# Two layers with feed-forwards in seven products: the weight ring's places given back after the products that read the slab itself, and the second layer's memory keys computed at two entries of the first layer

## The reference

```python
h = layer_norm(ALPHA * x + 0.5 * swiglu(x, ffn1_w_gu, ffn1_w_down), ...)      # feed-forward 1, d_ff 2816
... = split(h @ w_in)                                                         # 25 slabs of weights
o_dn, o_sw = deltanet_branch(...), sliding_window_attention(...)
o_xa = memory_cross_attention(xa_q, mem_n, w_mem_kv)   # k, v = split(mem_n @ w_mem_kv): keys and values
merged = sum(sigmoid(gates) * branches @ w_branch)
h = layer_norm(ALPHA * h + merged @ w_out, ...)
x = layer_norm(ALPHA * h + 0.5 * swiglu(h, ffn2_w_gu, ffn2_w_down), ...)      # feed-forward 2
```

## Time and profile before

| | |
|---|---|
| median of 3 runs | 3284.77 us (3282.89 to 3284.87) |
| the profiled execution's own time | 3286.88 us |
| its span in the trace | 3285.1 us |
| PE busy | 3029.7 us (92%) |
| DVE busy | 1937.5 us (59%) |
| ACT, POOL busy | 644.6 us (20%), 607.8 us (19%) |
| mean granted clock of PE | 0.985 of full speed |
| the two hybrid layers end | at about 1620 us |

### The profile page before, as it was taken

One profiled execution on the slowest core, in us unless ns is written; L12 is line 12 of the kernel. 1 busy time (PEld: TensorE's weight loads), 2 busy tenths in 40 slices (PEclk: granted clock), 3 DMA queues, 4 the chain that ended last, 5 costly groups with the idle time before them and its releaser, 6 DMA issues.

```text
span 3285.1 us, 34940 instructions
## 1 busy us (share of the span) xinstructions
PE 3029.7 (92%) x13098; PEld 2016.4 (61%) x13098; DVE 1937.5 (59%) x4473; ACT 644.6 (20%) x1581; POOL 607.8 (19%) x558
## 2 busy tenths in 40 slices
PE   8999999998999999999999888888989988888877
PEld 8947997894975899788586433333338643333322
DVE  7743533775763533310263877777766487777775
ACT  1113121110101223111154111111214421111110
POOL 0010000101001000000011433434421134444442
PEclk9999999999999999999999999999999999999999
DMA  5543223453443322364334999999993499999998
GB/s 222 180 153 129 103 90 128 154 182 139 169 178 141 128 90 103 141 236 161 115 116 181 421 422 421 412 415 419 412 402 116 155 422 421 420 413 418 415 415 354
DMA packets 114937, 830.38 MB, mean 253 GB/s; under 512 B 12880, under 2 KB 13136, under 8 KB 14160
## 3 DMA queue, kind: packets, MB, share of 16 engines
q0 software_dynamic: 73728, 536.90, 39.5%
q1 hardware_dynamic: 39456, 281.29, 23.6%
q10 hardware_dynamic: 1584, 9.95, 0.8%
HBM read 827.05 MB, written 1.05 MB: 252 GB/s over the span
## 4 chain that ended last, share of the span: by engine, by line
PE 64%; DMA 23%; DVE 8%; issue 5%; ACT 1%; POOL 0%; POOLq 0%; DVEq 0%; SPq 0%; ACTq 0%
DMA arena<-table_uv,idx 22%; PE bank L344 10%; PE bank L437 9%; PE bank L2404 8%; PE bank L491 6%; PE bank L679 5%; PE bank L371 4%; PE bank L424 3%; PE bank L915 3%; PE bank L2091 2%; PE bank L2276 2%; DVE arena L2985 1%; DMA ring<-stream 1%; DVE diag L2993 1%; PE bank L577 1%
## 5 line engine op out<-in xcount | busy, mean ns | idle before, releaser
L2404 PE MATMUL bank<-arena,diag 128*128 128x512 f32 x2048 | 1017.2, 623 | 189.6 <-DVE diag L2993 182.7
L2404 PEld LDWEIGHTS bank<-arena,diag 128*128 128x128 f32 x2048 | 360.2, 192 | 722.9 <-DVE diag L2993 457.4
L2985 DVE CUSTOM_DVE_ANT_0 arena<-arena 128x1024 f32<-128x1024 f32 x512 | 625.5, 1222 | 260.9 <-DMA arena<-table_uv,idx 257.4
L3069 POOL DMA_INDIRECT arena<-table_uv,idx x512 | 535.0, 1045 | 941.8 <-PE bank L2404 726.5
L1771 POOL TENSOR_TENSOR x_tok<-arena,ktail 128x1024 f32<-128x1024 f32 (+1 forms) x12 | 27.3, 2276 | 1571.3 <-ACT arena L943 1571.3
L2641 ACT ACTIVATE dots<-dots 128x1 f32<-128x1 f32 x512 | 103.8, 203 | 1089.8 <-DVE dots L2985 1089.4
L344 PE MATMUL bank<-x,ring 128*128 128x256 f32 x1440 | 316.9, 383 | 0.0
L344 PEld LDWEIGHTS bank<-x,ring 128*128 128x128 f32 x1440 | 276.2, 192 | 39.9 <-issue 1.9
L2993 DVE TENSOR_SCALAR diag<-cst,dots,soft 128x128 f32<-128x128 f32 x512 | 175.6, 343 | 0.0
L679 PE MATMUL bank<-x,ring 128*128 128x256 f32 x768 | 173.1, 379 | 0.0
L679 PEld LDWEIGHTS bank<-x,ring 128*128 128x128 f32 x768 | 143.2, 190 | 18.8 <-issue 1.0
(11 more groups left out here) (556 smaller groups left out, 4025.7 us busy)
## 6 DMA issues: line engine op xcount, KB each, us to landing
ring<-stream SPq DMA_DIRECT2D x258, 1024.0 KB, 4.8
arena<-table_uv,idx POOLq DMA_INDIRECT x512, 13.0
ktail<-ln_rows ACTq DMA_DIRECT2D x6, 1024.0 KB, 5.7
arena<-mem_rows SPq DMA_DIRECT2D x2, 1024.0 KB, 9.6
arena<-stream SPq DMA_DIRECT2D x2, 1024.0 KB, 6.8
sq<-keys ACTq DMA_DIRECT2D x2, 1024.0 KB, 4.8
cst<-consts SPq DMA_DIRECT2D x1, 1547.0 KB, 8.1
cst<-consts SPq DMA_DIRECT2D x1, 1089.0 KB, 14.1
```

The source lines that it names most:

```text
L2404: last = mm(bank[4 + 2 * tt + half][:, :], diag[:, n % DIAGS, :], row_slot(n)[:, D + 512 * half:D + 512 * half + 512], start=(h == 0 and k ...
L2985: v.tensor_tensor_reduce(u, u, tok[:, tt, :], 1.0, 0.0, ALU.mult, ALU.add, dots[:, tt, k:k + 1]).then_inc(u_used.sem, 1)
L3069: g.indirect_dma_start(out=row_slot(n), out_offset=None, in_=peer_uv, in_offset=bass.IndirectOffsetOnAxis(ap=idx[:, h % 2, tt, k:k + 1], a ...
```

## The change

1. **Up projection.** For j > 0 the product straight from the slab comes first in `both_tiles` and raises `slab_done` there; for j = 0 it is fourth. A new count, `gu_done`, is raised at the last of the five products; ACT's copy, and DVE's sums where they take a buffer over, wait for that in place of `slab_done`.
2. **Down projection.** The order within a slab is 1, 2, 3, then 6, 5, 7, 4, and `slab_done` is raised at product 3. In the tail, products 1, 2, 3 run slab by slab and give w = 8 and w = 9 back there; then 6, 5, 7, 4 run over the three slabs, and w = 10 is given back at product 5 of w = 8. The sums of w = 10 are waited for only before its product 6. Slab 0 keeps an order of its own (3, 2, 6, 7, 4, 1, 5). DVE, where it takes a down slab's buffer, waits for one slab more, since `slab_done` no longer says that the sums were read.
3. **Norm.** `norm_by_seven` takes the accumulators up in the new order (`ACC_AT`, `done`); its last wait is a count of its own, no longer the slab's.
4. **Keys of layer 1.** Their two slabs move in the stream: one ahead of layer 0's feed-forward 2, one ahead of layer 1's feed-forward 1. PE multiplies each there, into bank 7 (`next_keys`), ACT copies it out. Behind layer 1's feed-forward 1 the two slabs of values are left, with tile 1's transposes between them. The number of slabs is the same, so is the number of matmuls.

```diff
-FFN1_AT = 0
-MEM_AT = FFN1_AT + GU_SLABS + DOWN_SLABS
+FFN1_AT = (0, 2)
+MEM_AT = GU_SLABS + DOWN_SLABS
...
-FFN2_AT = OUT_AT + OUT_SLABS
+FFN2_AT = (OUT_AT + OUT_SLABS + 1, OUT_AT + OUT_SLABS)
...
+K_AHEAD_AT = (OUT_AT + OUT_SLABS, SLABS + 1)
+K_AHEAD_BANK = 7
+V_BANKS = ((2, 0), (1, 0))
...
                 def free(j):
+                    if j == W_X.index(K_AHEAD_BANK) and not first:
+                        pe.wait_ge(mem_evac.sem, mem_evac.at(1, 1 if l == 0 else 2))
...
+                    def of_slab():
+                        sum_ready(4)
+                        return product(out_y[:, 2 * P:3 * P], w[:, 3 * KC // 2:2 * KC, :], x_sum(4))
+
+                    if j > 0:
+                        of_slab().then_inc(slab_done.sem, 1)
                     product(out_y[:, 3 * P:4 * P], t_of(4), x[:, KC // 2:KC, P:T])
...
-                    product(out_x[:, 2 * P:3 * P], t_of(2), x_sum(2))
-                    sum_ready(4)
-                    product(out_y[:, 2 * P:3 * P], w[:, 3 * KC // 2:2 * KC, :], x_sum(4)).then_inc(slab_done.sem, 1)
+                    if j == 0:
+                        of_slab().then_inc(slab_done.sem, 1)
+                    product(out_x[:, 2 * P:3 * P], t_of(2), x_sum(2)).then_inc(gu_done.sem, 1)
...
+                for w in range(1, DOWN_SLABS - LAST):
+                    rows_ready(w)
+                    sums_ready(w)
+                    product(w, 1)
                     product(w, 2)
...
+                    product(w, 3).then_inc(slab_done.sem, 1)
+                    for i in (6, 5, 7, 4):
+                        product(w, i)
                 tail = range(DOWN_SLABS - LAST, DOWN_SLABS)
                 for w in tail:
-                    down_ready(w)
-                    last = product(w, 1)
-                last.then_inc(acc_done.sem, 1)
...
+                    rows_ready(w)
+                    if w < tail[-1]:
+                        sums_ready(w)
+                    for i in (1, 2, 3):
+                        last = product(w, i)
+                        if w == tail[-1]:
+                            last.then_inc(acc_done.sem, 1)
+                    if w < tail[-1]:
+                        last.then_inc(slab_done.sem, 1)
+                for i in (6, 5, 7, 4):
+                    for w in tail:
+                        if i == 6 and w == tail[-1]:
+                            sums_ready(w)
+                        last = product(w, i)
+                        if i == 5 and w == tail[0]:
+                            last.then_inc(slab_done.sem, 1)
+                    last.then_inc(acc_done.sem, 1)
...
+            def next_keys(s):
+
+                two_tiles(bank[K_AHEAD_BANK], slab(0, K_AHEAD_AT[s]), mem_n).then_inc(slab_done.sem, 1)
...
                 if seven_products(l, 1):
-                    ffn_by_seven(l, 1, FFN2_AT)
+                    next_keys(0)
+                    ffn_by_seven(l, 1, FFN2_AT[l])
+                    next_keys(1)
...
-                if i >= 3:
-                    dve.wait_ge(slab_done.sem, slab_done.at(l, slab - 2))
+                if i >= GU_SLABS + 3:
+                    dve.wait_ge(slab_done.sem, slab_done.at(l, slab - 1))
+                elif i >= 3:
+                    dve.wait_ge(gu_done.sem, gu_done.at(l, f * FC + i - 2))
...
                 by_channel(l, n, 0, x, gain, shift)
-                dve.wait_ge(slab_done.sem, slab_done.at(l, end))
+                done(7)
                 from_x(1, 0, acc(4))
```

More of the change, by code:

```diff
@@ L62 @@
 LN_BANK = 3
-ACC_AT = (0, 6, 9)
+ACC_AT = (0, 7, 10)
 def seven_products(l, f):
@@ new lines, in ffn_by_seven @@
+                sums_ready(0)
+                for i in (3, 2, 6, 7, 4):
+                    product(0, i)
+                pe.wait_ge(gu_summed.sem, gu_summed.at(l, f * FC + GU_SLABS))
+                product(0, 1).then_inc(slab_done.sem, 1)
+                product(0, 5)
+                for w in range(1, DOWN_SLABS - LAST):
+                    rows_ready(w)
+                    sums_ready(w)
+                    product(w, 1)
+                    product(w, 2)
+                    product(w, 3).then_inc(slab_done.sem, 1)
+                    for i in (6, 5, 7, 4):
+                        product(w, i)
@@ L557, in ffn @@
                 by_rows(l, 2 * f, hidden, FC, at + GU_SLABS, ready)
+            def next_keys(s):
+                two_tiles(bank[K_AHEAD_BANK], slab(0, K_AHEAD_AT[s]), mem_n).then_inc(slab_done.sem, 1)
             pe.wait_ge(x_loaded, 16)
             for l in range(DEPTH):
-                ffn_by_seven(l, 0, FFN1_AT)
+                ffn_by_seven(l, 0, FFN1_AT[l])
+                if l == 0:
+                    for s in range(2):
+                        w = slab(l, MEM_AT + s)
+                        two_tiles(bank[s], w, mem_n).then_inc(slab_done.sem, 1)
+                        if s == 0:
+                            x_waits(l, 0, 0)
+                            to_channels(l, 0, 1, y)
+                    pe.wait_ge(mem_evac.sem, mem_evac.at(l, 1))
                 for s in range(2):
-                    w = slab(l, MEM_AT + s)
-                    two_tiles(bank[s], w, mem_n).then_inc(slab_done.sem, 1)
-                    if s == 0:
+                    if l > 0 and s == 1:
                         x_waits(l, 0, 0)
                         to_channels(l, 0, 1, y)
-                pe.wait_ge(mem_evac.sem, mem_evac.at(l, 1))
-                for s in range(2):
                     w = slab(l, MEM_AT + 2 + s)
@@ L576, in tensor @@
                         for mt in range(TT):
-                            last = mm(bank[2 if mt == 0 else 0][:, :], mem_n[:, k, mt * P:mt * P + P],
+                            last = mm(bank[V_BANKS[l][mt]][:, :], mem_n[:, k, mt * P:mt * P + P],
                                       w[:, 4 * kk:4 * kk + 4, :].rearrange("p b n -> p (b n)"),
@@ L988, in ffn, with keys_of, next_keys @@
                 root_table()
+            def keys_of(s, b):
+                fn(kmem[:, 2 * s:2 * s + 2, :].rearrange("p h t -> p (h t)"), bank[b][:, :],
+                   ACT.Copy).then_inc(mem_evac.sem, 1)
+            def next_keys(s):
+                act.wait_ge(slab_done.sem, slab_done.at(0, K_AHEAD_AT[s] + 1))
+                keys_of(s, K_AHEAD_BANK)
             act.wait_ge(zeroed, 1)
```

116 lines of the change are left out of this document (52 added, 64 removed).

## The result

The changed kernel takes 3243.11 us in the median of 4 runs (3242.43 to 3243.71), the kernel before, run beside it, 3284.82 us (3282.89 to 3286.11). The ratio is 0.9872, 95% interval [0.9857, 0.9886]: 41.7 us less, where 39.5 were forecast.

A forecast was written before the change was run, and what follows sets the result against it. PE, with 64% of the chain, was taken to bound the kernel; 24.3 + 1.5 - 1.7 + 1.6 + 13.8 = 39.5 us off the 3285.1 us span gave 3245.6, forecast as 3245 us, range 3238 to 3260.

The forecast's parts named there:

- The tails, 24.3 us: Three down projection tails: PE's waits for DVE's sums and the slow stretch after them vanish, saving 24.3 us.
- Slabs behind the tails, 1.5 us: Keys behind two tails: places given back earlier let them start 0.89 us after the transposes, saving 1.5 us.
- Up projection, 0: Up projection: PE never waits in its steady part, so the earlier release saves 0.
- The entries, -1.7 and +1.6: Layer 0's feed-forward 2 entry 1.7 us longer, layer 1's feed-forward 1 entry 1.6 us shorter, keys included.
- the 4.74 I used: Slab ring: 4.74 us from a place given back until DVE can start on the new slab.
- The lock of DVE and POOL: Layer 1's entry: exclusive port lock keeps DVE's tile 1 addition ending as before; without it, some 0.75 us earlier.
- Behind layer 1's feed-forward 1, 13.8 us: After layer 1's feed-forward 1: two slabs of keys leave, 2 x 6.91 us, saving 13.8 us.
- The cover of 0.5 us for tile 1: Behind layer 1's feed-forward 1: ACT's tile 1 scaling takes 7.3 us, PE comes at 7.8; fits by 0.5 us.
- The signs that I named: Hybrid layers: no down projection waits, 18.0 us tails, clock near 1, entry waits 0.3 to 1 us, end near 1581.
- the release does not help: Rival, tails: sums of w = 10 stay the limit, the 24.3 us remain, 3269 us; chance 0.05.
- slower: Rival, up projection: turns DVE-bound; at 0.8 us wait for each of 63 slabs, 3295 us; chance 0.02.
- Part of it: Rival, entries: thinner cover, waits add up and PE's clock still falls; 3252 to 3262 us, chance 0.18.

The follow-up runs named there:

- POOL later: Against the changed kernel, POOL starts tile 1's token rows at the two entries only after DVE has written its half of `x`: 3252.93 us, ratio 0.9904.

## Why the prediction was right, step by step

- **The tails, 24.3 us**: measured 7.5 + 8.1 + 8.8 = 24.4 by starts. DVE's timeline of the changed kernel for slab 10 in the first tail, first and last sum:

```profile
203.55 0.69 DVE L1317 TENSOR_TENSOR z<-ring 128x512 f32<-128x512 f32 x1 [3.04 <-PE bank L503]
...
205.48 0.69 DVE L1322 TENSOR_TENSOR o_xa<-ring,z 128x512 f32<-128x512 f32 x1
```

  With t = 0 at 200.70 the sums run from 2.85 to 5.5 (forecast 2.6 to 5.3), for a use at 210.14, 9.4. The idle column alone would have given 14.6 plus the short waits of 2.1; reading start to start took in the slow stretch, and the runs bear that out. (The 0.857 us for a down product is not 48.08 divided by 56, which is 0.859; 21 products are 18.0 us either way.)
- **What in the change does it**: the prediction gave the steady part's release and the tail's order one term. The runs part them: the tail alone has all of it, the steady part alone leaves 2.5 us of wait three times. The early release of w = 7 wasn't needed, though by little: in the kernel with only the tail new DVE starts on slab 10 at 205.24, 0.2 us before PE reads it (205.47), where the forecast had 0.4.
- **Slabs behind the tails, 1.5 us**: 0.8 and 0.75, as forecast.
- **Up projection, 0**: shown by the kernel with it undone.
- **The entries, -1.7 and +1.6**: -2.0 and +1.3. The size of the waits was off in both. At the first, 0.6 and 0.5 us by starts in place of 0.46 and 0.35: the idle time is shorter than that, but the first row behind each wait is 0.1 us longer (2.05 and 1.16 in place of 1.95 and 1.06). At the second, the slab waited for took 1.3 us longer than the 4.74 I used (below), 1.68 us of wait in place of 0.46. It cost nothing: the slab only took the room of the two waits for DVE that I had put behind it, and the second `both_tiles` starts at 810.07, 20.4 us behind the transposes' start, as forecast. The missing 0.3 us lie inside that `both_tiles`, 4.72 us in place of 4.47; why is open.
- **The lock of DVE and POOL**, which I let hold tile 1's norm where it was: DVE's and POOL's timelines of the changed kernel at layer 1's entry:

```profile
788.82 2.23 DVE L1407 TENSOR_TENSOR arena<-arena 128x512 f32<-128x512 f32 x1
...
797.64 2.84 DVE L1320 TENSOR_TENSOR dec<-ring,dec 128x512 f32<-128x512 f32 x1
...
800.52 2.73 DVE L1322 TENSOR_TENSOR at_<-ring,dec 128x512 f32<-128x512 f32 x1
...
788.16 2.35 POOL L1811 TENSOR_TENSOR x_tok<-arena,ktail 128x1024 f32<-128x1024 f32 x1 [202.05 <-ACT arena L967]
```

  The addition to tile 1 starts 0.9 us earlier against the tail's end than in the earlier trace rows, takes 2.23 us in place of 1.35, and ends at 791.05, 1.40 us behind the transposes' start, where before it ended 1.42 behind it. Starting it sooner bought nothing: the forecast let it end where it did, and so it did. The Trainium skill, "SBUF — State Buffer", section "SBUF: two separate sides", describes this exclusive lock; the run with POOL later agrees with it (0.68 us for a sum without POOL, 2.74 and 2.83 beside it).
- **Behind layer 1's feed-forward 1, 13.8 us**: with the slab's 0.75 it makes 14.6, measured 14.7. The cover of 0.5 us for tile 1 held: the transposes at 1011.98 follow the values without a wait.
- **What the sum did not have**: 1.7 us of slow clock less from layer 0's tiny matmuls on, and 0.4 us more at the start, where the 24 matmuls of the program's first three `first_tile` took 8.15 us in place of 7.75. From the tiny matmuls to the transposes at layer 0's entry the kernel before took 326.5 us (255.94 to 582.39), the one with the keys alone too; the changed one took 324.8 (248.02 to 572.82), as did six others; the one with POOL later, the same code as the changed one up to there, took 323.1 (248.23 to 571.33). So this stretch moves in steps of 1.7 us without a change of code, and layer 1's, from the tiny matmuls to the end of the layers, does too: 561.7 us in the kernel before, the changed one and four others, 563.4 in the other four. I don't count the 1.7 us to the change. But in layer 0 the two kernels with the old tail and the old release, one trace each, are the two slowest, so the runs don't rule out that the change has a part in it.
- **How near the total came**: the trace ends at 3241.9, 3.7 us before the 3245.6 worked out. Nearly all of that lies outside the terms of the sum: 2.7 us come from the rest of the program and 1.7 from that slow clock, while the entries took 0.6 and the start 0.4 us more than forecast.
- **The signs that I named**: the waits at the third `first_tile` and before the second `both_tiles` were to be 0.3 to 1 us; they were 0.36 and 0.19 at the first entry, 1.68 and none listed at the second. The others came as named: 18.0 us in three tails, granted clock 1.00 at layer 1's entry, no wait between the values' slabs, the end of the layers at 1581.41.
- **Rivals**: "the release does not help" and "slower" are out by the tails' pace and by an up projection without waits but the one at the third slab, which was there before. "Part of it" named the right place, the entries, but its 7 to 17 us did not come: their sum is 0.6 us off the forecast.

## What to carry to other kernels

Where a ring is fed as its places come free, look at the last steps before the work changes its order: the steady loop had 4.3 us of slack here before the change (the sums of w = 7 were ready at 189.95, for a product at 194.27), and the tail, which asked for the sums of w = 10 two products after the slab was given its place, had none. Put there the products that need only the slab ahead of those that need something made from it; the early release in the steady loop and in the up projection could have stayed undone. Work that depends on nothing current costs a part of its weight (3.0 us for 12.1) if it goes where the engine waits anyhow, and gives back its full weight where it stood (14.7 us with the slab's 0.75). A lock between two engines can't be scheduled away by delaying one of them, if what the other does next meets it too and has less cover.

## What the runs showed of the hardware that was not expected

**A slab of 1 MB that took 6.0 us.** At layer 0's entry the slab behind the keys landed as usual. The transfers of the changed kernel from 583 to 591 us (engine, count, KB, us to landing):

```profile
ring<-stream SPq DMA_DIRECT2D x1, 1024.0 KB, 4.7
```

At layer 1's entry, from 796 to 806 us, it took 6.0 us, with one packet of the instruction queue in the same time (queue: packets, MB, share):

```profile
q8 instruction: 1, 0.02, 0.5%
...
ring<-stream SPq DMA_DIRECT2D x1, 1024.0 KB, 6.0
```

PE's wait for that slab was 1.64 to 1.77 us in five kernels and 1.07 and 1.49 in two others, and 0.28 to 0.45 at the other entry, so it goes with the place in the program and is no accident of one run. In all seven the slab took 5.4 to 6.1 us with such a packet in the same 10 us; with layer 1's keys left out it took 4.8, and the one packet of instructions in that window is of another queue. That the packet holds up one of the engines which carry the slab is my reading; no run took it away, and the trace shows that it can't be enough by itself. Of the 56 slabs of the changed kernel's layers (those of the program's start left out) that had a packet of this queue beside them, 15 took over 5.3 us; of the 155 without one, 9 did. The slab issued at 594.65 had one and took 4.7.

**Stalls and the clock.** Behind the six stalls of 4.7 to 5.0 us of the kernel before and of the one with the keys alone PE always went on at half pace; behind the three of 2.4 to 2.5 us in the kernel with only the steady part new, once. The length of a stall doesn't settle it. In the kernel with the early release alone PE went on at full pace behind 3.13 us (a row of 1.16 us) and fell to half pace about 1.5 us later (granted clock 0.62 from 588 to 592), but behind 2.51 us it was at half pace at once (2.08 us for a row that usually takes 1.06). In the kernel with POOL later two stalls of 1.59 us ended at half pace (2.08 and 1.93 us), where the kernel before went through stalls of 2.11, 2.39 and 2.42 us at full pace. What decides between these the runs don't show. For a forecast, a stall that is made shorter and not removed can still cost its slow stretch.
